# Attention of eight decode tokens over their cached keys: from key blocks as the stationary operand to query columns as the stationary operand

## The reference

```
def dilated_attn_sample(q, k_all, v_all, tab, window, dil):
    s = jnp.einsum('bthe,btkhe->bthk', q, kg, ...) * (HEAD_DIM ** -0.5)
    s = jnp.where(valid[:, None, :], s + bias, -jnp.inf)
    m = jnp.max(s, axis=-1)
    p = jnp.exp(s - m[..., None])
    l = jnp.sum(p, axis=-1)
    o = jnp.einsum('bthk,btkhe->bthe', p, vg...) / l[..., None]

def combine_groups(outs):          # z = l * exp(m - max m), o = sum(z * o) / sum(z)
```

## Time and profile before

| | |
|---|---|
| median of 3 runs | 2247.6 us (2247.16 to 2249.08) |
| the profiled execution | span 2250.2 us |
| PE busy | 2160.0 us, 96% |
| DVE, POOL, ACT busy | 877.7, 556.6, 510.9 us |
| chain of work that ended last | PE 90%, DVE 5% |
| mean granted TensorE clock | 0.969 |

### The profile page before, as it was taken

One profiled execution on the slowest core, in us unless ns is written; L12 is line 12 of the kernel. 1 busy time (PEld: TensorE's weight loads), 2 busy tenths in 40 slices (PEclk: granted clock), 3 DMA queues, 4 the chain that ended last, 5 costly groups with the idle time before them and its releaser, 6 DMA issues.

```text
span 2250.2 us, 33517 instructions
## 1 busy us (share of the span) xinstructions
PE 2160.0 (96%) x13052; PEld 2059.9 (92%) x13052; DVE 877.7 (39%) x1212; ACT 510.9 (23%) x796; POOL 556.6 (25%) x337
## 2 busy tenths in 40 slices
PE   5799899999899999999989999989999999999999
PEld 4799799999888888889989999979999999999999
DVE  8466667777223322232343444261221122211211
ACT  4466533333133332333310001031000000000000
POOL 3232232232311111111111123323333322233322
PEclk9899899999999999999997789989999999999999
DMA  3111022222432233224255334211111111111112
GB/s 123 40 40 48 29 79 75 93 82 86 151 132 89 89 113 117 80 89 139 81 207 222 104 132 149 88 35 47 47 37 47 47 47 47 47 47 47 47 45 87
DMA packets 71402, 188.39 MB, mean 84 GB/s; under 512 B 9257, under 2 KB 28668, under 8 KB 70652
## 3 DMA queue, kind: packets, MB, share of 16 engines
q1 hardware_dynamic: 41392, 136.97, 18.2%
q10 hardware_dynamic: 29964, 50.78, 6.2%
HBM read 145.06 MB, written 45.81 MB: 85 GB/s over the span
## 4 chain that ended last, share of the span: by engine, by line
PE 90%; DVE 5%; issue 1%; ACT 1%; DMA 1%; ACTq 0%; POOL 0%; SPq 0%; DVEq 0%; POOLq 0%
PE ups L456 62%; PE ups L556 12%; PE ups L576 6%; PE aux L599 3%; PE aux L643 1%; PE aux L480 1%; PE aux L621 1%; DVE ext L1066 1%; PE aux L507 1%; PE ups L587 1%; PE aux L587 1%; DVE ext L1062 1%; DVE big L1057 1%; DVE big_f L1051 0%; DVE big L1401 0%
## 5 line engine op out<-in xcount | busy, mean ns | idle before, releaser
L456 PE MATMUL ups<-big,wsp 128*128 128x344 f32 x9360 | 1528.3, 325 | 31.0 <-DVE big L1057 8.2
L456 PEld LDWEIGHTS ups<-big,wsp 128*128 128x128 f32 x9360 | 1501.9, 191 | 54.5 <-issue 26.4
L424 POOL CAST wsp<-wraw 128x1024 fp32r<-128x1024 f32 (+2 forms) x160 | 164.1, 1026 | 1611.6 <-issue 749.6
L426 POOL TENSOR_TENSOR wsp<-wraw,wsp 128x1024 fp32r<-128x1024 f32 (+2 forms) x160 | 380.6, 2379 | 12.8
L556 PE MATMUL ups<-big,wsp 128*128 128x344 f32 x1728 | 304.6, 328 | 6.9 <-ACTq L904 6.9
L556 PEld LDWEIGHTS ups<-big,wsp 128*128 128x128 f32 x1728 | 273.2, 190 | 12.2 <-ACTq L904 7.2
L1162 DVE RECIPROCAL x<-x 128x1024 f32<-128x1024 f32 x24 | 157.3, 6554 | 75.1 <-ACT x L864 75.1
L1209 DVE SCALAR_TENSOR_TENSOR x<-ups,ext 128x128 f32<-128x128 f32 (+1 forms) x192 | 58.7, 348 | 311.9 <-PE ups L576 230.7
L1398 DVE TENSOR_TENSOR ext<-ext,ups 128x1032 f32<-128x1032 f32 x22 | 27.0, 1229 | 373.3 <-PE ups L456 373.3
L576 PE MATMUL ups<-x 64*128 64x128 f32 (+1 forms) x384 | 132.3, 473 | 2.8 <-DMA ext<-bt_s 2.8
L1025 ACT ACTIVATE ext<-ups 128x1032 f32<-128x1032 f32 x22 | 22.7, 1031 | 489.9 <-PE ups L456 489.8
(11 more groups left out here) (180 smaller groups left out, 1168.0 us busy)
## 6 DMA issues: line engine op xcount, KB each, us to landing
wraw<-w_in SPq DMA_DIRECT2D x52, 512.0 KB, 3.3
wraw<-w_ffn_in SPq DMA_DIRECT2D x44, 512.0 KB, 3.2
x<-out_qkv SPq DMA_DIRECT2D x36, 512.0 KB, 4.5
out_qkv<-x ACTq DMA_DIRECT2D x32, 512.0 KB, 2.7
x<-gate_s SPq DMA_DIRECT2D x16, 516.0 KB, 4.2
wraw<-w_merge SPq DMA_DIRECT2D x16, 512.0 KB, 5.0
wraw<-w_ffn_out SPq DMA_DIRECT2D x16, 512.0 KB, 3.6
x<-o_s SPq DMA_DIRECT2D x8, 792.0 KB, 6.5
```

Of the source, the lines that this page charges most:

```text
L424: nc.gpsimd.tensor_copy(hi, raw).then_inc(w_hi, 1)
L426: nc.gpsimd.tensor_tensor(lo, raw, hi.bitcast(F32), ALU.subtract).then_inc(w_split[slot], 1)
L456: ins = nc.tensor.matmul(ups[:, slot, c, 0:CH], wsp[:, slot, w, k, :], src[:, a, k, c * CH:(c + 1) * CH], start=(k == 0 and w + a == 0), s ...
```

## The change

Keys and values become the moving operand. The queries of one group stand as 128 columns in four groups of 32 (one group for each pair of heads, 16 of its 32 columns in use: 8 sequences by 2 heads). One matrix product multiplies 32 query columns with 512 key columns (four sequences by 128 keys, or eight by 64), and its result goes to 32 partitions of PSUM. Four such products fill 128 rows; that is one `scores(r)`, and there are five, r = 0 to 4 (two for group 0, two for group 1, one for group 2). Each row then holds the scores of one head of one sequence against the keys of four or eight sequences; a mask takes out those of other sequences. One row of 2563 columns holds the scores of all three groups; it takes one maximum and one exp. `prob_columns(r)` transposes 512 of these columns, ACT copies them (`prob_copy`), and `values(r)` runs 16 products of 32 stationary columns by 128 moving columns, accumulated in PSUM four at a time. DVE adds up the five results (`s_values`), adds the tokens' own values (`s_rows`), and one transpose (`row_turn`) turns the rows back.

The order of PE's list is written anew, the loads of the cache wait for other counts and stand elsewhere in SP's list, DVE's `tokens(n)` is taken apart, and the first two units of `merge` run chunk by chunk in turns, each chunk waiting only for the tokens it reads. The core of the diff:

```diff
@@ SP
-                            sp.wait_ge(kv_used[n % 2], n // 2)
+                            sp.wait_ge(sm_pe, (5, 7, 8, 12)[n - 2])
...
-                    cache(2)
                     weights(2, 0)
-                    outputs(3)
-                    cache(3)
+                    cache(2)
+                    outputs(3)
                     weights(2, 1)
+                    cache(3)
                     outputs(4)
-                    cache(4)
                     weights(3, 0)
+                    cache(4)
...
                     outputs(6)
+                    cache(5)
                     outputs(7)
-                    cache(5)
@@ PE
+            def own_scores():
                 pe.wait_ge(sm_dve, 2)
+                for g in range(NG):
+                    ins = nc.tensor.matmul(aux[:, 0, g:g + 1], pm32[:, P * g:P * g + P], ones[:, 0:1], start=True, stop=True)
+                ins.then_inc(sm_pe, 1)
...
+            def scores(r):
+                g = r // 2
...
+                pe.wait_ge(sm_dve, (2, 4, 5, 6, 7)[r])
                 for f in range(4):
-                    for b in range(NB):
-                        at = 64 * g + 16 * f + 2 * b
-                        ins = nc.tensor.matmul(aux[0:NKEY[g], 1, at:at + 2], kc[g][:, b, f, :], qm[:, at:at + 2], start=True, stop=True)
-                ins.then_inc(kv_used[g % 2], 1)
+                    keys = kc[g][:, 4 * (r % 2):4 * (r % 2) + 4, f, :] if g < 2 else kc[g][:, :, f, :]
+                    ins = nc.tensor.matmul(aux[32 * f:32 * f + 32, 1, :], qm32[:, P * g + 32 * f:P * g + 32 * f + 32], keys,
+                                           start=True, stop=True)
+                ins.then_inc(sm_pe, 1)
+            def prob_columns(r):
+                pe.wait_ge(sm_act, 2)
+                pe.wait_ge(sm_dve, 8 + r)
+                for n in range(4):
+                    ins = nc.tensor.transpose(aux[:, 1, n * P:(n + 1) * P], srow[:, 512 * r + P * n:512 * r + P * n + P], ident[:])
+                ins.then_inc(sm_pe, 1)
+            def values(r):
...
+                pe.wait_ge(sm_act, 3 + r)
+                for n in range(4):
+                    for f in range(4):
+                        ins = nc.tensor.matmul(aux[32 * f:32 * f + 32, 1, 0:P], pts[:, n * P + 32 * f:n * P + 32 * f + 32],
+                                               vc[g][:, n if g == 2 else 4 * (r % 2) + n, f * P:(f + 1) * P],
+                                               start=(n == 0), stop=(n == 3))
+                ins.then_inc(sm_pe, 1)
...
-            y_chunks(2, 5)
+            y_chunks(2, 4)
+            own_scores()
+            scores(0)
+            y_chunks(4, 5)
             turn(0)
-            y_chunks(5, 6)
-            scores(0)
-            y_chunks(6, 7)
+            scores(1)
+            y_chunks(5, 7)
+            scores(2)
+            y_chunks(7, 8)
             turn(1)
-            y_chunks(7, 8)
-            scores(1)
-            y_chunks(8, 10)
+            y_chunks(8, 9)
+            scores(3)
+            y_chunks(9, 10)
+            scores(4)
+            y_chunks(10, 11)
             turn(2)
-            scores(2)
-            y_chunks(10, 13)
+            y_chunks(11, 13)
+            prob_columns(0)
...
             turn(7)
-            pe.wait_ge(ot_done, 9)
-            with pe.Fori(0, 4) as i:
+            row_turn()
+            for c in range(NCH):
+                pe.wait_ge(ot_done, 3 * c + 3)
+                for j in range(2):
+                    unit("merge", 0, j, big1, nk=4, parts=(c,))
+            with pe.Fori(1, 4) as i:
@@ ACT
+            def prob_copy(r):
+                act.wait_ge(sm_pe, 9 + 2 * r)
+                nc.scalar.activation(pts, aux[:, 1, :], ACT.Copy).then_inc(sm_act, 1)
             for n in range(1, 4):
                 weigh(n)
                 gate_load(n + 1)
                 gate_store(n)
             act.wait_ge(sm_max, 1)
-            nc.scalar.activation(srow, srow, ACT.Exp, bias=sstat[:, 1:2], accum_out=sstat[:, 2:3]).then_inc(sm_act, 1)
+            nc.scalar.activation(srow, srow, ACT.Exp, bias=st[:, 1:2], accum_out=st[:, 2:3]).then_inc(sm_act, 1)
             for n in range(4, 8):
                 weigh(n)
                 if n < 7:
                     gate_load(n + 1)
+                if n < 7:
+                    prob_copy((0, 2, 3)[n - 4])
+                if n in (4, 6):
+                    prob_copy((1, 4)[n // 2 - 2])
                 gate_store(n)
@@ DVE
             def s_norm():
+                for t in (qm32, pm32):
+                    nc.vector.memset(t, 0.0)
+                step.step(nc.vector.memset(v32, 0.0))
+                nc.vector.tensor_copy(by_row(v32), sqkv[:, 24:36, :].unsqueeze(3).broadcast_to([P, 12, NB, 2]))
...
+            def s_bias(r):
...
+                dve.wait_ge(sm_pe, 4 + r)
...
+                step.step(nc.vector.tensor_tensor(own, aux[:, 1, :].rearrange("p (b n) -> p b n", b=nb), line, ALU.add))
+                nc.vector.tensor_tensor(own, own, bmask[:, 4 * half:4 * half + nb].unsqueeze(2).broadcast_to([P, nb, n]),
+                                        ALU.add).then_inc(sm_dve, 1)
+            def s_max():
+                dve.wait_ge(sm_dve, 8)
+                step.step(nc.vector.tensor_reduce(st[:, 0:1], srow, AX_X, ALU.max))
+                nc.vector.tensor_scalar(st[:, 1:2], st[:, 0:1], -1.0, None, ALU.mult).then_inc(sm_max, 1)
...
-            tokens(0)
+            combine(0)
             s_norm()
-            tokens(1)
-            tokens(2)
-            s_scores()
-            tokens(3)
...
+            y_lru(0)
             s_own()
-            tokens(6)
-            tokens(7)
+            s_bias(0)
+            combine(1)
+            s_bias(1)
+            y_lru(1)
+            s_bias(2)
+            combine(2)
+            s_bias(3)
+            y_lru(2)
+            s_bias(4)
+            s_max()
+            combine(3)
+            y_lru(3)
+            combine(4)
+            s_values(0)
...
+            s_values(4)
+            combine(7)
+            s_rows()
+            y_lru(7)
+            split_turned(7)
             s_output()
-            split_turned(7)
```

More of the change, by code:

```diff
@@ L234, in build, with by_row @@
         vc = [kv[(g + 1) % 2][0:n, 0:NB * 512].rearrange("p (b f) -> p b f", b=NB) for g, n in enumerate(NKEY)]
[L235 to L246, removed]
+        vc[2] = kv[1][:, 0:4 * 512].rearrange("p (b f) -> p b f", b=4)
+        flat = ext[:, 0:3, :].rearrange("p a n -> p (a n)")
+        ROWS = 2560
+        srow, sbias, rsel = flat[:, 0:ROWS + NG], flat[:, 2563:2950], flat[0:HG, 2950:3078]
+        bmask = flat[:, 3078:3086]
+        sqs, rms, ul8 = flat[:, 0:192], flat[:, 192:384], flat[0:HG, 400:787]
+        qm32, pm32, oown = (tmp(4)[:, c] for c in (slice(136, 520), slice(520, 904), slice(904, 1032)))
+        pts = tmp(5)[:, 512:1024]
+        v32, hm = tmp(6)[:, 512:896], tmp(6)[:, 896:1024]
         osam = stc[:, 0:4, 0:NB]
+        def by_row(t):
+            return t.rearrange("p (a x) -> p a x", x=32)[:, :, 0:2 * NB].rearrange("p a (b h) -> p a b h", h=2)
         QT, KTT, VT = tmp(0)[:, 0:SEQ], tmp(1)[:, 0:SEQ], tmp(2)[:, 0:SEQ]
@@ L626, in score_rows, with own_values @@
+            def own_values():
+                pe.wait_ge(sm_dve, 13)
                 for g in range(NG):
-                    ins = nc.tensor.transpose(aux[0:ROWS, 1, g * P:g * P + NKEY[g]], sqs[0:NKEY[g], 64 * g:64 * g + 64],
-                                              ident[0:NKEY[g], 0:NKEY[g]])
+                    ins = nc.tensor.transpose(aux[:, 1, g * P:(g + 1) * P], v32[:, P * g:P * g + P], ident[:])
                 ins.then_inc(sm_pe, 1)
[L631 to L646, removed]
+            def row_turn():
+                pe.wait_ge(sm_dve, 14)
+                nc.tensor.transpose(aux[:, 1, 0:P], oown, ident[:]).then_inc(sm_pe, 1)
@@ L652, in turn @@
                     pe.wait_ge(ot_done, n)
+                else:
+                    pe.wait_ge(sm_dve, 3)
                 for k in range(4):
@@ new lines, in s_rows @@
+            def s_rows():
+                dve.wait_ge(sm_pe, 19)
+                dve.wait_ge(sm_dve, 13)
+                nc.vector.reciprocal(st[:, 3:4], st[:, 2:3])
+                for g in range(NG):
+                    step.step(nc.vector.scalar_tensor_tensor(oown, aux[:, 1, g * P:(g + 1) * P], srow[:, ROWS + g:ROWS + g + 1], oown,
+                                                             ALU.mult, ALU.add))
+                nc.vector.scalar_tensor_tensor(oown, oown, st[:, 3:4], hm, ALU.mult, ALU.mult).then_inc(sm_dve, 1)
@@ L1281, in s_output @@
             def s_output():
[L1282 removed]
+                dve.wait_ge(sm_pe, 20)
                 dve.wait_ge(out_done, 48)
[L1284 to L1288 removed]
+                step.step(nc.vector.tensor_reduce(osam, by_row(aux[:, 1, 0:P]), AX_X, ALU.add))
@@ L1338, in _ @@
                 dve.wait_ge(unit_done[j], T0["ylru"] + 1)
-            def tokens(n):
```

(30 more changed lines are left out.)

116 lines of the change are left out of this document (54 added, 62 removed).

## The result

The changed kernel took 2214.77 us (median of 4 runs, 2214.6 to 2218.81) against 2248.34 for the kernel before (4 runs, 2247.16 to 2249.78): a ratio of 0.9853, 95% interval 0.9839 to 0.9867, that is 33.6 us less. The forecast was 2232.0, range 2212 to 2246. The time lies in the range, near the end that the overlap of the column groups gave; the forecast itself gave less than half of the gain. The profiled execution of the changed kernel has a span of 2217.0, 33.2 less than before; its own time, 2218.81, is the longest of the four.

A forecast was written before the change was run, and what follows sets the result against it. PE's own instruction list was taken to bound the stage. Work removed -72.8, new PE work +38.2 and waits +19.0 gave -15.6 us: 2234.6 from the profiled span, 2232.0 for the runs' median, range 2212 to 2246.

The forecast's parts named there:

- the price of the ten runs: New score and value runs on PE: 3.45 us each at the streaming price, five of each kind, 34.5 us together.
- the row with wide moving operands: Profile row of fp32 products with 344 streamed columns, two instructions each: 0.29 us an instruction, 0.843 ns a column.
- the first rival: Score and value runs: column groups overlap between successive products, 14.5 us less, 2217.5 us; chance 0.36 (2208 to 2222).
- its stronger form: Score and value runs: all four column groups side by side, up to 26 us less, about 2210 after handshakes with DVE.
- (b): `prob_columns(0)` waits for the exp on ACT: 4.5 us, and 2.5 for the clock, 7.0 together.
- (a): `own_scores` behind y3 waits for DVE's `s_norm`: PE idles 6.5 us, and 2.5 for the lower clock, 9.0 together.
- (c): `scores(r+1)` needs `s_bias(r)`: nothing, or 1 us behind a `combine`; `turn(7)` and `row_turn` wait 1.8 us.
- (d): End of stage: third unit of `merge` waits 4.9 us for its weights, 2.5 for the clock: 7.4 in place of 6.2.
- What was removed (72.8): Old PE work: value runs 31.4, score runs 24.5, own scores 0.8, clock loss 15.3, small transposes and `hm` product 0.8 us.
- The clock behind the runs: Lower granted clock slows the chunks behind the six old score and value runs: 15.3 us in all.
- The forecast's "now and then" instruction of DVE: A DVE instruction that now and then takes 1.85 us too long (2.54 for 0.69), allowed for in the exp's wait.

The follow-up runs named there:

- one, two and four column groups: Changed kernel with all products of a set written to one or two column groups in place of four: 2240.1 and 2223.34 us, against 2214.77 with four.
- the exp ahead: Changed kernel with the exp of the row moved ahead of `weigh(3)` in ACT's list: 2217.98 us, ratio 0.9858.
- The kernel with one group: Changed kernel with all products of a set written to the same 32 partitions of PSUM: 2240.1 us, ratio 0.9953.
- Three moves: Changed kernel with exp and `prob_copy(0)` earlier on ACT, `own_scores` and score runs later, `merge` weights ahead of side tiles, PE's order rewritten: 2199.3 us, ratio 0.9783.

## Why the prediction was right or wrong

The step that failed is the price of the ten runs: "a `scores(r)` is ... 3.45 us" and "a `values(r)` ... 3.45". Measured were 1.0 and 1.0. The prediction took the row with wide moving operands, in which every product uses all 128 columns, and from it that products advance one at a time. For 32 columns in one group that price is right within 5% (3.55 and 3.61); what it could not show is that products of different column groups run side by side. That was the first rival, in its stronger form: all four at once. It had 0.36 as a whole, and "about 2210" for that form; the runs showed 2214.77, since other terms came out larger (below). That the time fell within the range is owed to the low end that this rival had given it, not to the price that the forecast chose. Rows that show a price at one shape spoke for it with more weight than they had, since none of them could have shown the overlap.

The Trainium skill (TensorEngine Tiling (Array Packing), Key Properties) says that tiles work independently and can load and multiply in parallel. The trace agrees, with 3.55, 1.84 and 0.99 us for one, two and four column groups.

Step by step, as shares of the difference in the profiled execution (the forecast for it was -15.6, measured -33.2):

| step | forecast, us | measured, us | difference |
|---|---|---|---|
| five score runs | 17.3 | 5.9, of it 0.9 of low clock in the first | -11.4 |
| five value runs | 17.3 | 5.05 | -12.2 |
| first work behind a run | 0 | some 0.18 for each of nine | +1.6 |
| twenty transposes of probabilities | 2.2 | 3.3, of it 0.7 of low clock behind (b) | +1.1 |
| `own_scores` | 1.0 | 1.44 at the lower clock | +0.4 |
| (a) wait; clock of the chunk behind | 6.5; 2.5 | 6.9; 1.1 | -1.0 |
| (b) wait; clock of the chunk behind | 4.5; 2.5 | 6.5; 2.1 | +1.6 |
| (c) small waits | 1.8 | 3.2 (1.4, 0.8, 0.5, 0.5) | +1.4 |
| (d) third unit of `merge`: wait and clock | 7.4 | 3.4 and 1.7 | -2.3 |
| `wo`: wait for the last row, clock behind | 0 | 4.3 and 2.25 more than before | +6.5 |
| waits for the split between `merge` and `wo` | 0 | 2.1 in place of 3.7 | -1.7 |

The differences sum to -16.0, so -31.6 with the forecast's -15.6. The stage also began 1.5 us earlier than in the execution of before, which makes -33.1, against -33.2 measured. The ten runs alone would have given 23.6 us more than forecast; the other rows took 7.6 of it back. The clock's part of (d) is worked out from 144 products at 0.158 us (3.79 for 24), 22.75, against 24.45 in the chain; that of `wo` from the 555 products behind it, 89.88 us against 87.63.

What was removed (72.8) was sized rightly as far as it can be tested: cutting the old runs out of the kernel before gave 58.7 us, and 61.7 follow from the forecast's terms with the new waits that came. The clock behind the runs, 15.3 us of it, was a real cost and is gone.

(a) was right in place, cause and size: 6.9 us against 6.5, for `s_norm`. (b) was right in place and cause, and 2 us short; with the exp ahead the wait moved to the copy that ACT does behind it, which the forecast had not named as next in line. (c) holds: no wait of several microseconds stands before a `scores` or `values`. (d) was right in place and cause and too large by 2.3; it did not foresee that the last merged row would be late for `wo`. The last rows of `merge` pass through DVE, ACT and DVE again, and in this execution two of DVE's instructions there took about 3.2 us, as the timeline shows (start us, us, line, operation, shapes [idle before <-releaser]; POOL's split of the weights of `wo` in the second block):

```profile
1334.72 3.29 DVE L1431 SCALAR_TENSOR_TENSOR big<-ext,big 128x1032 f32 x1 [1.46 <-ACT big L1056]
1337.94 1.22 DVE L1427 SCALAR_TENSOR_TENSOR x<-x,ups 128x1032 f32<-128x1032 f32 x1
1339.29 3.17 DVE L1429 TENSOR_TENSOR ext<-x 128x1032 f32<-128x1032 f32 x1
1343.99 1.23 DVE L1431 SCALAR_TENSOR_TENSOR big<-ext,big 128x1032 f32 x1 [1.52 <-ACT big L1056]
```

```profile
1334.55 2.37 POOL L427 TENSOR_TENSOR wsp<-wraw,wsp 128x1024 fp32r<-128x1024 f32 x1
1336.86 2.05 POOL L425 CAST wsp<-wraw 128x1024 fp32r<-128x1024 f32 x1
1339.00 2.38 POOL L427 TENSOR_TENSOR wsp<-wraw,wsp 128x1024 fp32r<-128x1024 f32 x1
```

Others of the same shape take 1.23. Each of the two begins 0.2 to 0.3 us after an instruction of POOL and ends 1.1 us after that one ends (1336.92 and 1338.01; 1341.38 and 1342.46), as if it had begun its work only then. In `merge` of both kernels the same distance, 1.08 to 1.10 us, shows at every instruction of these two lines (L1429 and L1431; before, L1372 and L1374) that took over 0.2 us too long, thirteen in all. The DVE instruction between the two (L1427), which has one operand in PSUM, keeps its 1.22 beside POOL's. So the long instructions come with POOL's split of weights; what the two engines share isn't shown, and no run moved the split away. Without the two, the row would have been ready some 4 us earlier and the wait would be near nothing. The spans of the other three runs, 2212.8 to 2213.0, are 4 us shorter, which fits this, but no trace of those runs shows it, so that part stays argued. The forecast's "now and then" instruction of DVE (2.54 for 0.69) lies beside POOL's split in the same way: it began at 1176.88, behind one of POOL from 1176.53 to 1178.88, and ended 0.54 after it.

The kernel with one group is the forecast's own case, with runs of 3.55 and 3.61. By the forecast's sum it should gain 14.3 us (15.6, less 1.3 for the runs' length); it gained 10.6 by its ratio (6.7 to 14.2). So the rest of the sum was about 4 us too favourable, hardly beyond the noise, and in any case by less than the 24 us that the price of the runs was too high.

## What to carry to other kernels

Where several small stationary operands share one moving shape, count the column groups first: a set spread over four groups costs little more than a quarter of the same set in one, and no row of a kernel that uses full width can show that. When PE gets much shorter work in a stage, sum up what the other engines must have done by each point of its list, since their chains become the waits. Before a wait is taken away, look what stands next in the same chain: 6.5 us taken away came back as 7.0 at the next step, 3.4 as 5.7, and 6.0 as 5.3. Three moves that gave 2.5, 6.3 and 1.6 us alone gave 15.7 with PE's order rewritten for them; each of these figures is good to some 4 us, so it isn't shown that together they are worth more than their sum. And where a late row or a late exp comes from long DVE instructions, look whether POOL works beside them.

## What was not expected of the hardware

Four column groups run nearly fully side by side: 3.55 us in one group against 0.99 in four is a factor of 3.6, with fp32 products of two instructions each, four groups reading the same 128 rows of the array.

The first full-width work behind a run of 32-column products takes some 0.18 us more: 3.96 to 4.00 us for a chunk that takes 3.79 behind a turn, with one, two or four groups. It isn't the chunk's own: where a turn follows the run, the turn pays, as the chain of the kernel with all three moves shows:

```profile
1250.14 1.01 PE aux L656 x32
1251.15 0.62 PE aux L679 x4
...
1252.27 3.78 PE ups L468 x24
```

The turn (L679) takes 0.62 in place of 0.44, and the chunk 3.78. The Trainium skill (TensorEngine Tiling (Array Packing), Key Properties) says that a change of tiling mode drains the engine; the trace fits this, with 0.18 us, but nothing here tells a drain from another cost of the change.

The granted clock was 0.63 in the first old run, in which two columns are streamed for each load, and 0.50 behind it, though PE was busy all the time. It was 1.00 in and behind runs of 3.55 us that stream 512 or 128 columns through 32 columns of weights; no run here has such products for as long as the old 11 us. In the stage of the changed kernel it is low only behind an idle PE.
